# ScalarE's copies of transposed groups without their wait for v, a final norm on 128 partitions, and a new order of the first expert loads

## The reference, cut to what matters

```
x_n = rmsnorm(h, ln1_g);  pr, pk, pv, cb, cc, ch, ga, gb = split(x_n @ w_in)
r, k, v = shift_mix(pr), shift_mix(pk), shift_mix(pv)
S_t = S_{t-1} diag(w_t) + (S_{t-1}(-kk_t))(kk_t * a_t)^T + v_t k_t^T;  y_t = S_t r_t   # 8 heads of 64
h = h + (sigmoid(ga) * rwkv(y) + sigmoid(gb) * conv(cb, cc, ch)) @ w_o
h = h + moe(rmsnorm(h, ln2_g))      # 32 experts, top 4, clamped SwiGLU, blocks of rows
out = rmsnorm(h, lnf_g)[16:]        # the 16 meta rows are dropped
```

## Time and profile before

| what | us |
|---|---|
| median of the runs | 2924.07 |
| profiled execution, its own time | 2926.43 |
| its span, from first to last instruction | 2924.8 |
| TensorE busy | 2721.9 (93%) |
| VectorE busy | 1860.8 (64%) |
| ScalarE busy | 1321.8 (45%) |
| granted TensorE clock, mean over the span | 0.966 |
| one `w_hi` piece on ScalarE, mean | 1.92 |
| one `w_lo` piece on VectorE, mean | 2.28 |

### The profile page before, as it was taken

The page is one execution under the profiler, slowest core; times in us unless marked ns, Lnnn a source line. Parts: engine busy times, 40 slices in busy tenths (PEclk is TensorE's granted clock), DMA queues, the critical chain, the costliest instruction groups (busy, mean ns, idle before and its releaser), DMA issues.

```text
span 2924.8 us, 55470 instructions
## 1 busy us (share of the span) xinstructions
PE 2721.9 (93%) x21131; PEld 2315.9 (79%) x21131; DVE 1860.8 (64%) x2116; ACT 1321.8 (45%) x1427; POOL 498.3 (17%) x528
## 2 busy tenths in 40 slices
PE   7999999999898999898499999999999999999994
PEld 6787877879798999876377777777778888888883
DVE  3474757676422111244566666767689999999996
ACT  2303113131221111133356655656567777777775
POOL 1010101010000000112423223232222222122220
PEclk9999999998999999999699999999999999999997
DMA  4000000000011112142467768677699999999998
GB/s 110 22 2 9 15 2 22 2 23 2 15 43 51 44 43 65 54 117 70 182 249 268 264 249 287 253 263 279 249 382 384 378 381 380 381 380 381 381 381 282
DMA packets 143643, 536.88 MB, mean 184 GB/s; under 512 B 17905, under 2 KB 71511, under 8 KB 90557
## 3 DMA queue, kind: packets, MB, share of 16 engines
q1 hardware_dynamic: 123005, 492.74, 45.0%
q0 software_dynamic: 20544, 42.74, 5.8%
HBM read 501.01 MB, written 34.42 MB: 183 GB/s over the span
## 4 chain that ended last, share of the span: by engine, by line
PE 83%; DVE 5%; DMA 5%; issue 4%; ACT 2%; SPq 0%; POOL 0%; DVEq 0%; POOLq 0%; ACTq 0%
PE bank L880 32%; PE bank L2063 12%; PE bank L2065 12%; PE bank L2064 12%; PE bank L2072 4%; DMA raw_first<-in_w_e_down 3%; PE bank L876 2%; PE bank L2041 2%; PE bank L2099 1%; PE bank L1975 1%; PE bank L1977 1%; PE bank L1976 1%; PE bank L2051 1%; DVE nrm L775 1%; PE bank L931 1%
## 5 line engine op out<-in xcount | busy, mean ns | idle before, releaser
L1890 DVE TENSOR_TENSOR w_lo<-raw_first,w_hi 128x2048 fp32r<-128x2048 f32 x275 | 619.0, 2284 | 75.0 <-ACT w_hi L1667 74.9
L1667 ACT ACTIVATE w_hi<-raw_first 128x2048 fp32r<-128x2048 f32 x276 | 529.6, 1919 | 212.9 <-DMA raw_first<-in_w_e_up 56.8
L2063 PE MATMUL bank<-w_hi,x_hi 128*128 128x512 f32 x1088 | 434.8, 400 | 2.4 <-ACT yo_rows L1715 2.4
L2065 PE MATMUL bank<-w_hi,x_lo 128*128 128x512 f32 x1088 | 426.0, 392 | 0.0
L2064 PE MATMUL bank<-w_lo,x_hi 128*128 128x512 f32 x1088 | 425.5, 391 | 0.0
L1890 DVE TENSOR_TENSOR w_lo<-raw_rest,w_hi 128x2048 fp32r<-128x2048 f32 x136 | 308.6, 2283 | 16.4 <-ACT w_hi L1667 16.3
L1667 ACT ACTIVATE w_hi<-raw_rest 128x2048 fp32r<-128x2048 f32 x136 | 260.9, 1919 | 118.6 <-PE bank L2099 44.3
L880 PE MATMUL bank<-xm_hi,ring_hi 128*128 128x260 f32 x896 | 261.6, 292 | 17.1 <-DVE dz L832 8.2
L880 PE MATMUL bank<-xm_hi,ring_lo 128*128 128x260 f32 x896 | 254.9, 284 | 0.0
L880 PE MATMUL bank<-xm_lo,ring_hi 128*128 128x260 f32 x896 | 254.8, 284 | 0.0
L2063 PEld LDWEIGHTS bank<-w_hi,x_hi 128*128 128x128 f32 x1088 | 205.4, 189 | 52.0 <-issue 10.5
(11 more groups left out here) (381 smaller groups left out, 4660.4 us busy)
## 6 DMA issues: line engine op xcount, KB each, us to landing
raw_first<-in_w_e_up SPq DMA_DIRECT2D x138, 1024.0 KB, 6.1
raw_first<-in_w_e_gate SPq DMA_DIRECT2D x70, 1024.0 KB, 6.4
raw_rest<-in_w_e_gate SPq DMA_DIRECT2D x70, 1024.0 KB, 4.8
raw_first<-in_w_e_down SPq DMA_DIRECT2D x68, 1024.0 KB, 7.1
raw_rest<-in_w_e_down SPq DMA_DIRECT2D x68, 1024.0 KB, 8.3
ring<-in_w_in SPq DMA_DIRECT2D x40, 512.0 KB, 4.0
hn_d<-hn SPq DMA_DIRECT2D x10, 416.0 KB
h_d<-h_all SPq DMA_DIRECT2D x10, 416.0 KB
```

The lines of the kernel that those rows point to most:

```text
L1667: nc.scalar.activation(w_hi[:, j % NRING, :, :], raw_piece(j), ACT.Copy).then_inc(hi_done, 1)
L1890: nc.vector.tensor_tensor(w_lo[:, j % NRING, :, :], raw_piece(j), w_hi[:, j % NRING, :, :].bitcast(f32), ALU.subtract).then_inc(lo_done, 1)
L2063: nc.tensor.matmul(ps[:, :], hi, w_hi[:, slot, k, :], start=start and k == 0, stop=False)
L2065: ins = nc.tensor.matmul(ps[:, :], lo, w_hi[:, slot, k, :], start=False, stop=stop and k == HK - 1)
```

## The change

Three edits. In the recurrence ScalarE's wait for v ahead of the twelve copies is gone; on TensorE a wait for `kh` is set ahead of k's transposes (it has one for `bh` ahead of b's, and one for v ahead of v's). At the start of the experts SyncE loads two pieces, waits for the first gathered rows and then loads the other four; ScalarE and VectorE treat the rows after two split pieces. At the end the 1024 rows that are wanted are held in 8 tiles of 128 partitions, eight consecutive rows to a partition; they are read in four transfers of two tiles (8 KB runs, 32 KB apart) and written in eight (4 KB runs, 32 KB apart). The scale row is broadcast to 128 partitions.

```diff
-            dve_j.done(act, 'v', j)
...
-                if x == 'v':
-                    dve_j.done(pe, 'v', j)
+                if x in 'kv':
+                    dve_j.done(pe, 'kh' if x == 'k' else 'v', j)
...
-    fss = sb("fss", [TP, NT])
-    frs = sb("frs", [TP, NT])
+    FT = (TOK - META) // 128
+    h_fin = Plan(nc, shared['start'])("h_fin", [128, FT, D])
+    fss = sb("fss", [128, FT])
+    frs = sb("frs", [128, FT])
...
         for j in range(NRAW):
+            if j == 2:
+                sp.wait_ge(rows_in[0], 16)
             load_now(e0, j)
...
-        sp.dma_start(gf_b, lnf_g.partition_broadcast(TP)).then_inc(gf_in, 16)
+        sp.dma_start(gf_b, lnf_g.partition_broadcast(128)).then_inc(gf_in, 16)
...
-        for t in range(NT):
-            sp.dma_start(h_all[:, t, :], h_d[TP * t:TP * (t + 1), :]).then_inc(tile_got[t], 16)
-        for t in range(NT):
+        h_parts = h_d[META:TOK, :].rearrange("(p t) c -> p t c", t=FT)
+        for t in range(0, FT, 2):
+            sp.dma_start(h_fin[:, t:t + 2, :], h_parts[:, t:t + 2, :]).then_inc(tile_got[t], 16)
+        out_parts = out.rearrange("(p t) c -> p t c", t=FT)
+        for t in range(FT):
             sp.wait_ge(fin_done, t + 1)
...
+            sp.dma_start(out_parts[:, t, :], h_fin[:, t, :]).then_inc(out_done, 16)
...
-        for j in range(NRING):
+        for j in range(2):
             split_hi(j, 16, j)
         for f in range(4):
             x_hi_part(0, f, True)
+        for j in range(2, NRING):
+            split_hi(j, 16, j)
...
-        for t in range(NT):
-            act.wait_ge(tile_got[t], 48 if t == 0 else 32)
+        for t in range(FT):
+            if t % 2 == 0:
+                act.wait_ge(tile_got[t], 48 if t == 0 else 32)
...
-        for j in range(LEAD):
+        for j in range(2):
             split_lo(j, j)
         for f in range(2):
             x_lo_part(0, f, True)
+        for j in range(2, LEAD):
+            split_lo(j, j)
```

More of the change, by code:

```diff
@@ L1280, in experts_program @@
     row_ov = ex("row_ov", [128, 2], u32)
-    fin_junk = ex("fin_junk", [TP, D])
-    gf_b = ex("gf_b", [TP, D])
+    fin_junk = ex("fin_junk", [128, D])
+    gf_b = ex("gf_b", [128, D])
     assert ex.at <= 229344, ex.at
@@ L1431, in on_sync @@
         sp.sem_inc(sp_passed, 1)
-        for t in range(NT):
-            sp.dma_start(h_all[:, t, :], h_d[TP * t:TP * (t + 1), :]).then_inc(tile_got[t], 16)
-        for t in range(NT):
-            sp.wait_ge(fin_done, t + 1)
[L1436 to L1440, removed]
+        h_parts = h_d[META:TOK, :].rearrange("(p t) c -> p t c", t=FT)
[3 more added lines that the diff above has]
+        for t in range(FT):
+            sp.wait_ge(fin_done, t + 1)
+            sp.dma_start(out_parts[:, t, :], h_fin[:, t, :]).then_inc(out_done, 16)
+        sp.wait_ge(out_done, 16 * FT)
         for s in range(NRAW):
@@ L1740, in on_scalar @@
                             x_hi_part(r + 1, X_WIDE.index(j), wide)
-        for t in range(NT):
-            act.wait_ge(tile_got[t], 48 if t == 0 else 32)
+        for t in range(FT):
+            if t % 2 == 0:
+                act.wait_ge(tile_got[t], 48 if t == 0 else 32)
             if t >= 1:
                 act.wait_ge(fsq_done, t)
-            nc.scalar.activation(fin_junk, h_all[:, t, :], ACT.Square, accum_out=fss[:, t:t + 1]).then_inc(fsq_done, 1)
+            nc.scalar.activation(fin_junk, h_fin[:, t, :], ACT.Square, accum_out=fss[:, t:t + 1]).then_inc(fsq_done, 1)
             act.wait_ge(fsq_done, t + 1)
-            nc.scalar.activation(frs[:, t:t + 1], fss[:, t:t + 1], ACT.Sqrt, bias=eps_t[0:TP, :], scale=1.0 / D
+            nc.scalar.activation(frs[:, t:t + 1], fss[:, t:t + 1], ACT.Sqrt, bias=eps_t[:, :], scale=1.0 / D
                                  ).then_inc(fstd_done, 1)
@@ L1958, in finish @@
             dve.wait_ge(frs_done, t + 1)
-            nc.vector.scalar_tensor_tensor(out=h_all[:, t, :], in0=h_all[:, t, :], scalar=frs[:, t:t + 1], in1=gf_b,
+            nc.vector.scalar_tensor_tensor(out=h_fin[:, t, :], in0=h_fin[:, t, :], scalar=frs[:, t:t + 1], in1=gf_b,
                                            op0=ALU.mult, op1=ALU.mult).then_inc(fin_done, 1)
-        for t in range(NT):
+        for t in range(FT):
             finish(t)
```

## The result

The median fell from 2924.71 us (2923.67 to 2930.89, four runs) to 2891.81 us (2889.40 to 2895.04, four runs). The two medians lie 32.9 us apart; the ratio, estimated from the same runs, is 0.9874, 95% interval 0.9858 to 0.9891, that is 36.8 us less (31.9 to 41.5). The two profiled executions, spans 2924.8 and 2889.8 us, lie 35.0 us apart.

A forecast was written before the change was run, and what follows sets the result against it. Waits on the path bound it: ScalarE's for v, TensorE's for gathered rows, and the final transfers. Gains 10.6 + 1.7 + 7.4 + 8.0 = 27.7 us take the 2924.07 us median to 2896.4 us, range 2889 to 2908.

The forecast's parts named there:

- the clock's part of edit 1: Recurrence: without the idle stretch TensorE's clock may not fall; 3.4 us at most, 1.7 taken, bounds -2 and +3.4.
- the end: Last reads and writes: 128-partition tiles move at about 400 GB/s, span's end near 2916.2; worked out 8.6 us, taken 8.0.
- The wait's own price: Recurrence: ScalarE's copies start 2.66 us earlier in each of four columns, 10.6 us in all, lower end 8.2.
- the fall might come at a dearer place: Recurrence: the clock falls elsewhere at more cost; in the rival of small copy gains, 4 us, time about 2904.7, chance 0.08.
- The rows: Start of experts: gathered rows land at 1418.2 instead of 1425.6, a gain of 7.4 us, bounds 5.6 and 8.1.
- zeroing and padding hold the gather's issue: Start of experts: GpSimd's zeroing and padding still keep the gather's issue at 1413.47.
- The slack for piece 2: Start of experts: piece 2's low part ready at 1430.7, wanted at 1434.6, so 3.9 us of slack.
- The first tile and the pace on VectorE: End: first tile done at 2900.0, then 1.39 us a tile on VectorE, seven more by 2909.8.
- The lower end: End: gain of 5.4 us if reads keep the old per-engine rate (273 GB/s, 15.4 us), stride harmless.
- that rival: Strided tail at the end: both directions at 221 GB/s, costing 7 us there, time 2911.4 us; chance 0.12.
- A microsecond won "stays won": Recurrence and start of experts: gains there persist, since what follows goes by relations, not by events of fixed time.
- The range: Whole kernel: time between 2889 and 2908 us; the likeliest case's own range 2891 to 2904.

The follow-up runs named there:

- Edit 1 alone: Kernel before with only the recurrence change (ScalarE's wait for v gone, TensorE's wait for `kh` added): ratio 0.9942, 17.0 us less.
- x1_pads: Changed kernel with GpSimd's zeroing and padding writes moved between the gather of 128 rows and that of the extra rows: ratio to before 0.9876.
- The run with the wait alone: Kernel before with only SyncE's wait for the gathered rows, old order on ScalarE and VectorE: first product 29.8 us after the first load, against 27.9.
- edit 3: As a run: kernel before with only the end changed to 8 tiles of 128 partitions: ratio 0.9940, 17.6 us less.
- the filling: Kernel before, ScalarE's wait for v kept, 20 unused transposes on TensorE ahead of its third group of b: ratio 0.9976, 7.0 us less.

## Why the prediction fell short, by its own steps

Two terms of the sum failed: the clock's part of edit 1, put at 1.7 us, and the end, put at 8.0 us. The mechanisms of all three edits held.

- **The wait's own price, 2.66 us a column:** right. The copies start 0.05 us after the last copy for v, v and `kh` are covered, and overlap slowed nothing (sets of 1.82 us).
- **The clock's part, "I take half":** this is the term of edit 1 that was mis-sized. I had worked out 0.84 us a column and discounted it because the fall might come at a dearer place. Measured: 0.81 to 0.91 a column with the wait kept and the idleness filled, 3.4 us in sum where I took 1.7, and 3.5 us a column in all four columns of each kernel without the wait, so 14.1 us in place of 12.3. Edit 1 alone was timed at 17.0 us less (13.2 to 21.1), which leaves 12.3 out. The caution was right about a single execution, whose columns gain 9 to 20 us; the mean over six executions (14.4 us, known to about 4) can't tell the whole term from half of it. The rule of the Trainium skill ("TensorE: Matmul & The Clock Gate", Part 1), by which the sum would have held the whole 3.4 us, did better; the traces of this place agree with it.
- **The rows, 7.4 us:** 7.0. The landing was sized at 4.7 us and took 5.3. That zeroing and padding hold the gather's issue was right by 0.45 us only: the indices themselves take 7.05 us to come (x1_pads). The slack for piece 2 held. The run with the wait alone shows that without the new order on ScalarE and VectorE the gain is lost and 2 us more; I had not priced that half.
- **The end, 8.0 us:** the second mis-sized term. It measured 10.9 us, both in the pair of profiles and as the mean of six profiles with the old end (34.0 us, 30.4 to 36.7) less that of nine with the new (23.2 us); against single old executions it is 7 to 14 us. The first tile and the pace on VectorE were right (7.96 us from the first read's issue to the first scale, by the sum 8.14, and 1.39 us a tile). The rate was 421 GB/s, not 400, and it, not VectorE, set the end, as worked out: the transfers were over near 2888.2, 21.7 us after the first read's issue, where the sum had 23.2. From there to the span's end it took 1.6 us, not 2.3, and I had rounded 8.6 down to 8.0. The lower end was wrong as well: reads of 15.4 us in place of 10.5 would have left 8.6 - 4.9 = 3.7 us, not 5.4. The stride cost nothing: that rival falls, for steps of 32 KB. The rule on the number of engines stands in the Trainium skill, "DMA: Bandwidth & Descriptors", section "Why a DMA increments its semaphore by 16 and not by 1", not in the one that I named; the DMA shares of 0.83 and 1.0 agree with it, but the rate of the old reads was lower than it alone would make it.
- **A microsecond won "stays won":** nothing speaks against it. Rounds took 1461.3 and 1469.3 us in two profiles of the changed kernel, 1464.9 and 1468.8 in two of before. The 3.6 us of the first pair lie within that scatter, and so do the -2.1 us between the columns and the first load (632.2 to 636.8 us in the fourteen profiles whose first load is not held back).
- **The range:** with 14.1 + 7.0 + 10.9 = 32.0 us of gains in the three places themselves, the forecast was 4.3 us short by its terms; another 3.0 us of the 35.0 between the profiles came from places where nothing had changed. I made the sum against one execution (2926.43 us), while in later sets of runs the same kernel had medians of 2927 to 2933. The range had room for the terms, hardly any for this.

What stays open: what makes one execution's columns 615 and another's 624 us, beyond that the clock falls at more places in the long ones; why tiles of 104 partitions read at 15 to 22 GB/s an engine and write at 26; and why edit 3 and the filling timed 6.7 and 3.6 us better than their places. The three edits alone sum to 41.9 us against 36.8 together; with intervals of 3 to 5 us to each side that is no contradiction, and nothing was found in the traces that would be counted twice.

## What to carry to other kernels

When a wait leaves TensorE idle, price the slow stretch after it as part of the wait: fill the idleness with work that isn't used and see what the following steps then take. When a transfer is to come first, look at what was issued before it on any queue, small index transfers included, and reorder the engines that consume it together with the queue, or the gain turns into a loss. Give tiles that only move data all 128 partitions.

## What the runs showed of the hardware that was not expected

- A transfer of 1 KB landed 7 us after its issue beside 2 MB of weights, and within 3 us without them; a gather of 512 KB took 9.6 us behind two pieces of weights that were issued 0.7 us before it, and 4.4 us with nothing ahead.
- Reads of 104-partition tiles of 4 KB rows ran at 197 to 290 GB/s in six executions of the same code, of 128-partition tiles at 400 to 425, whatever the run and the stride. The DMA share was 0.84 and 1.0, so each engine that took part was also slower, 15 to 22 against 26 GB/s. Writes of 104 partitions ran at 26 GB/s an engine, like those of 128.
- The same 1342 matmuls of a column took 160.6 to 164.9 us in the changed kernel, at mean granted clocks of 0.97 to 0.94; edit 1 alone had two columns of 163.82 us, one after the other.
- After the same 1.6 us of idleness in 4 us the granted clock stayed at 1.00 over the next 8 us in one column and was 0.79 in the next.
